# Four dense stages and their norms joined into two blocks, with the norm done by token halves

## The reference, cut to what matters

```python
def layer_norm(x, g, b):
    mu = jnp.mean(x, -1, keepdims=True)
    var = jnp.mean(jnp.square(x - mu), -1, keepdims=True)
    return (x - mu) * lax.rsqrt(var + 1e-5) * g + b
...
x = layer_norm(ALPHA * x + mixer(x) @ w_out, g0, b0)
u = causal_dwconv(x @ w_up)
x = layer_norm(ALPHA * x + (gelu(u1) * u2) @ w_down, g1, b1)
```

## Time and profile before

| | |
|---|---|
| time, three runs | 2137.26, 2137.46, 2151.37 us; median 2137.46 |
| the profiled execution | 2151.56 us, its span 2149.8 us |
| mean granted TensorE clock | 0.912 |
| busy, share of the span | TensorE 90%, weight loads 81%, VectorE 48%, ScalarE 31%, GpSimd 11% |
| DMA | 152.42 MB, 71 GB/s over the span |

### The profile page before, as it was taken

One profiled execution on the slowest core, in us unless ns is written; L12 is line 12 of the kernel. 1 busy time (PEld: TensorE's weight loads), 2 busy tenths in 40 slices (PEclk: granted clock), 3 DMA queues, 4 the chain that ended last, 5 costly groups with the idle time before them and its releaser, 6 DMA issues. The chain is left out here.

```text
span 2149.8 us, 31699 instructions
## 1 busy us (share of the span) xinstructions
PE 1937.1 (90%) x13190; PEld 1750.6 (81%) x13190; DVE 1031.1 (48%) x1718; ACT 669.7 (31%) x1288; POOL 236.2 (11%) x388
## 2 busy tenths in 40 slices
PE   8998998896999999996998969788779699999996
PEld 8986665595999999986798958555478699999995
DVE  6555553235666662226463133336652566665223
ACT  4632442224333332114353220111121533333112
POOL 0110000000222220000100010123000122221000
PEclk9995898798999999998999977668789899999998
DMA  5203700011222222213112230100221222222221
GB/s 183 68 20 98 247 1 2 20 60 59 89 79 85 83 77 81 82 35 101 60 63 75 79 121 1 44 0 1 89 81 38 88 79 89 80 80 83 82 76 57
DMA packets 51329, 152.42 MB, mean 71 GB/s; under 512 B 7394, under 2 KB 17058, under 8 KB 50546
## 3 DMA queue, kind: packets, MB, share of 16 engines
q1 hardware_dynamic: 51186, 150.40, 21.6%
HBM read 138.12 MB, written 16.39 MB: 72 GB/s over the span
## 5 line engine op out<-in xcount | busy, mean ns | idle before, releaser
L674 PE MATMUL ps<-x_high,w_high 128*128 128x288 f32 x2288 | 689.5, 301 | 62.2 <-DVE x_low L696 60.9
L675 PE MATMUL ps<-x_low,w_high 128*128 128x288 f32 x2288 | 681.6, 298 | 0.0
L676 PE MATMUL ps<-x_high,w_low 128*128 128x288 f32 x2288 | 679.2, 297 | 0.0
L674 PEld LDWEIGHTS ps<-x_high,w_high 128*128 128x128 f32 x2288 | 435.4, 190 | 70.1 <-issue 51.6
L653 DVE TENSOR_TENSOR w_low<-w_raw,w_high 128x1024 fp32r<-128x1024 f32 (+1 forms) x215 | 253.7, 1182 | 428.9 <-ACT w_high L648 428.7
L676 PEld LDWEIGHTS ps<-x_high,w_low 128*128 128x128 f32 x2288 | 437.2, 191 | 0.0
L675 PEld LDWEIGHTS ps<-x_low,w_high 128*128 128x128 f32 x2288 | 436.4, 191 | 0.3
L648 ACT ACTIVATE w_high<-w_raw 128x1024 fp32r<-128x1024 f32 (+1 forms) x215 | 221.5, 1032 | 529.3 <-PE ps L676 455.6
L674 PE MATMUL ps<-g_high,w_high 128*128 128x288 f32 x704 | 211.1, 300 | 1.7 <-ACT ub L761 1.7
L675 PE MATMUL ps<-g_low,w_high 128*128 128x288 f32 x704 | 207.7, 295 | 0.0
L676 PE MATMUL ps<-g_high,w_low 128*128 128x288 f32 x704 | 206.9, 294 | 0.0
(11 more groups left out here) (399 smaller groups left out, 2497.9 us busy)
## 6 DMA issues: line engine op xcount, KB each, us to landing
w_raw<-in_w_up SPq DMA_DIRECT2D x88, 512.0 KB, 3.6
w_raw<-in_w_odd SPq DMA_DIRECT2D x36, 512.0 KB, 3.4
w_raw<-in_w_down SPq DMA_DIRECT2D x32, 512.0 KB, 3.5
w_raw<-in_w_even SPq DMA_DIRECT2D x19, 512.0 KB, 3.5
ptok<-in_cache_tok SPq DMA_DIRECT2D x32, 192.0 KB, 2.6
w_raw<-in_w_down SPq DMA_DIRECT2D x16, 384.0 KB, 3.2
w_raw<-in_w_mix SPq DMA_DIRECT2D x16, 384.0 KB, 3.1
w_raw<-in_w_mix SPq DMA_DIRECT2D x8, 512.0 KB, 3.7
```

The source lines that it names most:

```text
L674: pe.matmul(out, self.high[:, s, k, :], high(k0 + k)[:, cols], start=first, stop=False)
L675: pe.matmul(out, self.high[:, s, k, :], low(k0 + k)[:, cols], start=False, stop=False)
L676: mm = pe.matmul(out, self.low[:, s, k, :], high(k0 + k)[:, cols], start=False, stop=last)
```

## The change

`dense_early` puts the first mix projection, its norm, the first feed-forward with its norm and the odd layer's projection into one block with one weight stream of three slots; `dense_late` does so for the second mix and feed-forward (four slots of 6 inner blocks for the mix, whose end the second stream waits for). The semaphore clears move: one before each of these blocks and one before the scans. Gains and biases of all norms are loaded once, at the start.

`PostNorm` takes the place of `ProjectAndNorm` and `FinishX`:

- The first `opening` output tiles (3 in the first mix, 2 in the second, 1 in the down projections) are multiplied together, inner block by inner block.
- A pivot, the mean of output tile 0's 128 features per token, made by two matmuls on ones, is taken off every tile as it comes. GpSimd adds the tiles and their squares up feature by feature; the mean of squares less the square of the mean is the variance.
- The last `tail` output tiles (3, 2 and 1) are multiplied first for token half 0, then for half 1, and hold their weights until then.
- `sums` turns the two running sums into columns of one number per token (tokens along the partitions) with matmuls of one moving column, twelve per half; variance, root and reciprocal work on [128, 3]; `spread` lays the reciprocal and mean times reciprocal back along the tokens in PSUM with six matmuls against the identity. Both stand at fixed places in TensorE's order.
- The next stage's first three tiles are opened by halves (`open_next`): tiles 0 and 1 for half 0 as the inner blocks are normalised, then tile 2, then all three for half 1. All three chunks are released at the end.
- `y` is stored by halves.

```diff
+    def open_next(self, pe, m0):
+        for k in range(KD):
+            if k == 3:
+                self.sums(pe, 1)
+            pe.wait_ge(self.low_done, k + 1)
+            for m in range(2):
+                wt.landed_for(pe, m0 + m, k)
+                wt.step(pe, m0 + m, k, 2 * m, 0, net.high, net.low)
+        self.spread(pe, 1)
+        wt.multiply_half(pe, m0 + 2, 4, 0, net.high, net.low)
+        for k in range(KD):
+            pe.wait_ge(self.low_done, KD + k + 1)
+            for m in range(3):
+                mm = wt.step(pe, m0 + m, k, 2 * m, 1, net.high, net.low)
+                if k == KD - 1:
+                    mm.then_inc(wt.used, 1)
...
+            def between(k):
+                at = (m - self.n) * kt + k
+                if at == 5:
+                    self.sums(pe, 0)
+                elif at == 13:
+                    self.spread(pe, 0)
...
+    LATE = {3: (-1, 1, 4), 2: (0, 4), 1: (3,)}
+    FRESH = {3: (0, 1, 4), 2: (1, 2, 4), 1: (0, 1, 3)}
...
+        self.variance(dve, 0)
+        self.late(dve, -1)
+        self.deviation(dve, 0)
+        for k in range(KD + 2):
+            self.normalise(dve, 0, k)
+            self.late(dve, k)
+            if k == 6:
+                self.variance(dve, 1)
+        self.deviation(dve, 1)
+        for k in range(KD + 2):
+            self.normalise(dve, 1, k)
+
+    def late(self, dve, at):
+        for j, when in enumerate(self.LATE[self.tail]):
+            if when == at:
+                self.wt.product_out(dve, self.m0 + self.n + j)
+                self.residual(dve, 1, self.n + j)
+        if self.fresh:
+            for j, when in enumerate(self.FRESH[self.tail]):
+                if when == at:
+                    self.fresh.split_low(dve, self.f0 + j)
...
+    def normalise(self, dve, a, k):
+        if k == 0:
+            dve.wait_ge(self.spread_done, a + 1)
+        if k < KD:
+            dve.tensor_tensor(x(k), x(k), net.ps[:, 7, 0:HT], ALU.mult).then_inc(self.scaled, 1)
+        if 1 <= k <= KD:
+            dve.wait_ge(self.scaled, KD * a + k)
+            dve.tensor_tensor(x(k - 1), x(k - 1), net.ps[:, 6, 0:HT], ALU.subtract).then_inc(self.normed, 1)
+        if k >= 2 and self.fresh:
+            dve.wait_ge(self.x_done, KD * a + k - 1)
+            dve.tensor_tensor(net.xl[:, k - 2, self.half(a)], x(k - 2), net.xh[:, k - 2, self.half(a)].bitcast(F32), ALU.subtract).then_inc(self.low_done, 1)
...
+            pool.wait_ge(self.added, at_least)
+            pool.tensor_tensor(self.sum1[:, cols], self.sum1[:, cols], net.x[:, m, cols], ALU.add)
+            pool.tensor_tensor(self.sum2[:, cols], self.sum2[:, cols], sq[:, m % 2, cols], ALU.add).then_inc(self.added, 1)
...
+        for i in self.wt.ahead():
+            self.wt.split_low(dve, i)
+            norm(k + 1)
+            self.parts.split_low(dve, k)
+            k += 1
...
+        wt = SplitWeights(net, 3, 8, (io["w_mix0"], KD, 8), (io["w_up"][0], 2 * FM, KD), (io["w_down0"], KD, FM), (io["w_odd"], OddProject.M, KD))
...
             def _(sp):
+                ffn.load_small(sp)
+                mix.on_sync(sp)
+                ffn.on_sync(sp)
+                odd.on_sync(sp)
```

More of the change, by code:

```diff
@@ L658, in ahead, with chunk_of @@
         return range(min(lo, len(self.chunks)), min(hi, len(self.chunks)))
-    def multiply(self, pe, m, out_bank, high, low, ready=None):
[L662 to L669, removed]
-                for a in range(2):
[L671 to L677, removed]
+    def chunk_of(self, m, k):
+        i, n = self.tiles[m][0], self.chunks[self.tiles[m][0]][3]
+        return i + k // n, k % n
@@ new lines, in landed_for, with step @@
+    def landed_for(self, pe, m, k):
+        i, at = self.chunk_of(m, k)
+        if at == 0:
+            pe.wait_ge(self.low_done, i + 1)
+    def step(self, pe, m, k, out_bank, a, high, low):
+        i, at = self.chunk_of(m, k)
+        s, kt = i % self.slots, self.tiles[m][2]
+        out, cols = self.net.ps[:, out_bank + a, 0:HT], slice(HT * a, HT * a + HT)
+        pe.matmul(out, self.high[:, s, at, :], high(k)[:, cols], start=(k == 0), stop=False)
+        pe.matmul(out, self.high[:, s, at, :], low(k)[:, cols], start=False, stop=False)
+        return pe.matmul(out, self.low[:, s, at, :], high(k)[:, cols], start=False, stop=(k == kt - 1))
@@ new lines, in chunk_end @@
+    def chunk_end(self, m, k):
+        i, at = self.chunk_of(m, k)
+        return at == self.chunks[i][3] - 1
+    def multiply(self, pe, m, out_bank, high, low, ready=None):
+        for k in range(self.tiles[m][2]):
+            self.landed_for(pe, m, k)
+            if ready is not None:
+                ready(pe, k)
+            for a in range(2):
+                mm = self.step(pe, m, k, out_bank, a, high, low)
+            if self.chunk_end(m, k):
+                mm.then_inc(self.used, 1)
@@ new lines, in sums @@
+    def sums(self, pe, a):
+        net, tail = self.net, self.tail
+        pe.wait_ge(self.c_done, KD + a * tail)
+        pe.wait_ge(self.added, KD - 2 + a * (tail - 1))
+        pe.wait_ge(self.squared, KD + a * tail)
+        slot = (KD - 1) % 2
+        for i, (run, last) in enumerate(((self.sum1, net.x[:, KD - 1, :]), (self.sum2, self.sq[:, slot, :]))):
+            for j in range(3):
+                t, col = self.stat_cols(a, j), 3 * i + j
+                out = net.ps[:, a, col:col + 1]
+                pe.matmul(out, run[:, t], net.inv_d, start=True, stop=False, skip_group_check=True)
+                mm = pe.matmul(out, last[:, t], net.inv_d, start=False, stop=True, skip_group_check=True)
+        mm.then_inc(self.summed, 1)
@@ L1200, in _ @@
             def _(sp):
-                for i in range(len(wt.chunks)):
-                    wt.load(sp, i)
-                proj.on_sync(sp)
+                ffn.load_small(sp)
+                mix.on_sync(sp)
+                ffn.on_sync(sp)
+                odd.on_sync(sp)
             @block.tensor
             def _(pe):
-                proj.on_tensor(pe)
+                mix.norm.on_tensor(pe)
+                ffn.on_tensor(pe)
+                odd.on_tensor(pe)
+            @block.gpsimd
@@ L1209, in _ @@
+            def _(pool):
+                mix.norm.on_gpsimd(pool)
+                ffn.on_gpsimd(pool)
+                odd.on_gpsimd(pool)
             @block.scalar
             def _(act):
[L1211 to L1217 removed]
+                mix.on_scalar(act)
+                ffn.on_scalar(act)
+                odd.on_scalar(act)
```

1074 lines of the change are left out of this document (619 added, 455 removed).

## The result

The kernel after takes 2120.48 us (median of four runs, 2118.03 to 2122.15) beside 2144.41 of the kernel before on the same chip: ratio 0.989, 95% interval 0.984 to 0.994, some 24 us. On a second chip the medians were 2120.28 and 2146.37; a few executions there were slower as a whole at a lower granted clock, and without them, as in every ratio of this document, it is 0.983 (0.976 to 0.991), some 36 us. 46 were forecast. The kernel is faster and its time lies in the stated range; the size of the gain was missed.

What follows compares the result with a forecast made beforehand. TensorE, busy 90% of the span, bounds the kernel; its time beyond the matmul stream falls from 177.5 to 132.2 us, plus 1.4 ahead of the scan: 46.7 saved, scaled from median 2137.46 to 2091 us, range 2062 to 2128.

Steps and rivals of the forecast that it cites:

- The prices of the new work: In the norms: column sums 2.4 us a pass, spread 1.9, VectorE's normalising op 0.40 in sequence.
- The waits before the fourth tile: At each boundary: TensorE waits for slot release, copies, convolution and weight split: 3.9 us, 6.2 into the odd layer.
- The first mix's opening waits: First mix: 8.1 us kept, barrier 1.3, small loads 1.0; then third chunk 3.6, slots and residual 3.1.
- The second mix and its boundary: Second mix 17.7 against 19.4 us; boundary into the second up projection 24.0 against 34.2.
- the end: From the last product to the span's end: 22.5 us beyond the stream, against 28.2.
- I take nothing, bounds 0 and 10 us in all: Projections: GpSimd's 576-wide adds nearly fit a mix tile's 6.4 us and cost nothing; bounds 0 and 10 us.
- the first boundary: Into the first up projection: 21.4 us beyond the stream (14.5 + 3.9 + 3), against 34.4.
- half clock 1.6: First mix opening: 1.6 us lost to TensorE's half clock.
- clock 3: Each boundary: 3 us lost to a lowered clock at two waits, bounds 0 to 7.
- the odd boundary: Into the odd layer: 15.9 us, 6.2 before tile 3 and clock 3; sum 25.1 against 33.8.
- The third rival: Boundaries and mix openings: clock stays at 0.50, costing 84 us, so 2174 us; chance 8%.
- The first rival: Openings give back half the gain: VectorE at 0.52 per op, column sums at upper price; 28 us, 2119; chance 18%.

Runs made afterwards that it cites:

- split-first run: Kernel after, with the fourth tile's weight chunk split ahead of the first tile's copies and convolution in the feed-forwards and odd projection: 2114.0 us.
- one-column run: Kernel after, with GpSimd's running sums cut to one column from the third tile on, all waits and other work kept: median 2116.11 us.

## Why the prediction was right and wrong

**Held.** The prices of the new work. Four passes of column sums and two spreads, as windows of the kernel after:

```profile
484.51:489.62 5.11, 5.11 (x25) 5.11 (x25) 0.00 (x0) 0.05 (x1) 0.00 (x0) 0.50 0.00 0
...
935.14:937.74 2.60, 2.60 (x26) 2.60 (x25) 0.00 (x0) 0.93 (x1) 0.00 (x0) 1.00 0.00 0
957.67:962.64 4.97, 4.97 (x25) 4.97 (x25) 0.74 (x3) 1.39 (x3) 0.00 (x0) 0.50 0.00 2
1638.60:1641.19 2.59, 2.59 (x26) 2.59 (x25) 0.00 (x0) 0.00 (x0) 0.00 (x0) 1.00 0.00 0
495.19:496.44 1.25, 1.25 (x14) 1.25 (x13) 0.00 (x0) 0.00 (x0) 0.05 (x1) 1.00 0.00 0
968.11:969.37 1.26, 1.26 (x14) 1.26 (x13) 0.00 (x0) 0.00 (x0) 0.00 (x0) 1.00 0.00 0
```

The sums take 2.60 at full clock (2.4 forecast, bounds 0.8 to 4.9, and 5.0 to 5.1 where the clock is 0.50), a spread 1.25 (1.9). VectorE's normalising op takes 0.45 (0.40 in sequence was forecast; two in a row start 0.37 apart). The waits before the fourth tile, 3.79, 5.95 and 3.79, stood in the prediction as 3.9, 6.2 and 3.9, and the split-first run shows the cause that it gave. The first mix's opening waits, 10.0, 2.2 and 3.1, were forecast as 10.4, 3.6 and 3.1. The second mix and its boundary saved 12.3 of 11.9, the end 9.0 of 10.8.

**Failed, and the largest term: "I take nothing, bounds 0 and 10 us in all" for GpSimd.** The step compared totals, 3.6 us of GpSimd and 2.7 of VectorE in a tile's 6.4. But no add can run before the pivot, and the pivot stands behind tile 3; so the adds of four tiles, and the splits and centrings that they slow, fall into the time of the last full tile and the half tiles, and TensorE asks for the sums at the end of exactly that. Cost: 8.2 us, where the first boundary misses 10.9 in all, shown by the one-column run; and it is the opening with three tiles that causes it, shown by the run with one. An earlier pivot alone does not help (wait 3.1), since the last full tile's residual, centring and square then come late. That the bound held 8.2 doesn't help: the value taken was its lower end.

Rows agree here with what the Trainium skill (SBUF — State Buffer, Who interferes with whom) says, that the one of the two that comes second stands still until the first is done: the centring that begins at 476.92 has 0.46 us of work and ends at 478.13, 0.32 behind the end of GpSimd's add at 477.81, while the residual at 476.44, which reads PSUM, takes its 0.44 beside the same add. The prediction named the rule and then added shares of a tile's time, as if the two could divide it; each wait is as long as what the other has left.

**Failed, smaller: "half clock 1.6" in the mix opening and "clock 3" per boundary.** In the first mix the granted clock averages 0.81, and 0.85 with the one-tile opening. The opening's 192 matmuls, and two stretches at the lower level that begin toward the end of the waits of 3.1 and 3.7:

```profile
423.52:460.63 37.11, 31.80 (x193) 31.28 (x194) 12.71 (x15) 8.11 (x11) 0.00 (x0) 0.82 0.29 85
450.39:457.21 6.82, 5.82 (x24) 5.82 (x25) 3.59 (x5) 1.06 (x1) 0.00 (x0) 0.50 0.53 156
484.52:494.76 10.24, 10.24 (x45) 10.24 (x46) 1.64 (x7) 1.73 (x4) 1.07 (x2) 0.50 0.00 0
```

The opening is busy for 31.8 us where its stream is 25.6: half clock cost 6.2 there and not 1.6. These 4.6 and the 8.2 of the adds make 12.8 more than forecast; the rest of the first boundary came out about 2 better. Around the odd boundary, where 5.8 us are missing, the second pass of sums ran at 0.50 (4.97 instead of 2.4) and so did most of the 24 matmuls behind the first pass (4.96 instead of 3.2); that is 4.3 of the 5.8, and the prediction's 3 us were for two waits. The third rival (the clock does not come back) named the mechanism, but it stayed at a few us per boundary.

**A rival that fits by number alone.** The first rival's 2119 is within 2 us of the result. Its mechanism, VectorE at 0.52 an op and all column sums at the upper price, is not what the rows show: VectorE is at 0.45, and six of the eight passes of column sums take 2.6 to 3.0, near the price that was taken and not the upper one. The match is luck.

**Not in the sum at all.** The forecast scaled the profiled execution to a median, as if one run's difference were a factor. It is not: the attention and the scans of the same program wander by 20 and 17 us, each about as much as the 18 us that the touched stretches miss. The median of three runs from which the forecast went, 2137.46, was itself 7 below the median with a fourth run, 2144.41; that makes the miss in the time, 29 us (2091 to 2120.48), look larger than it is. The measured time also lies just above 2116, the limit under which the prediction, with 75%, called the kernel faster.

## What to carry to other kernels

An engine's adds are not hidden because they fit the time per tile; ask when the first of them may start and when the last is asked for, and add up what lies between. An opening that takes several tiles together saves on paced input and makes the weight slots, the residuals and the statistics of those tiles come due at one time: here it cost 13.5 us more than one tile after the other (10.8 at the least). When stretches that nobody edited move by as much as the change is worth, compare the edited stretches of two profiles and leave the whole times for the end.

## What the runs showed of the hardware that was not expected

- The same instructions took 408 to 428 us (attention) and 287 to 304 us (scans) in fourteen profiles, the scans with a mean granted clock of 0.67 to 0.75; VectorE, ScalarE and GpSimd were busy for the same time to within 0.5 us in each scan that is shown.
- The clock fell to 0.50 in the midst of a stretch in which TensorE never waited, 0.8 us behind a pass of column sums (938.50, above).
- Matmuls with one moving column are slowed by the clock like full ones: a pass of the twelve takes 2.60 us at 1.0 and 4.97 at 0.5.
- In the kernel after, GpSimd's 576-wide add takes 1.43 us by itself and up to 2.20 beside a VectorE op that reads two operands from SBUF; VectorE's op of 0.46 becomes 1.20 and the one of 1.22 becomes 2.44.
